# Two transformer blocks on one core: other waits at four stage entries, the GLU's second mean taken of raw squares, and the last norm's weight multiplied before its root is there

## What is computed

```python
def second_block(x, ...):                       # x: (1, 512, 1024)
    h = rms_norm(x, norm_mix_pre)               # x itself is the first block's final rmsnorm
    q, k, v, glu_in, gates = split(h @ w_in)
    a = dilated_attention(q, k, v, rel_bias)    # 3 groups of 4 heads, merged
    c_val, c_gate = split(glu_in)
    c = causal_depthwise_conv(c_val * sigmoid(c_gate), 31 taps)
    c = silu(layer_norm(c))
    mixed = g_a * (a @ w_attn_out) + g_c * (c @ conv_pw_w)
    x = x + rms_norm(mixed @ w_out, norm_mix_post)
    h = rms_norm(x, norm_ffn_pre)
    u = causal_depthwise_conv(h @ w_up, 3 taps)
    f = gelu(u_gate) * u_val
    return x + rms_norm(f @ w_down, norm_ffn_post)

def rms_norm(x, g):
    return x * rsqrt(mean(x * x) + 1e-6) * g
```

## Time and profile before

| | us |
|---|---|
| median of 3 runs | 1909.72 |
| lowest and highest | 1908.21, 1918.91 |
| the profiled execution's own time | 1913.29 |
| its span, first to last instruction | 1911.6 |
| PE busy in the span | 1864.7 (98%) |
| mean granted TensorE clock | 0.991 |

### The profile page before, as it was taken

The page is one execution under the profiler, slowest core; times in us unless marked ns, Lnnn a source line. Parts: engine busy times, 40 slices in busy tenths (PEclk is TensorE's granted clock), DMA queues, the critical chain, the costliest instruction groups (busy, mean ns, idle before and its releaser), DMA issues.

```text
span 1911.6 us, 24566 instructions
## 1 busy us (share of the span) xinstructions
PE 1864.7 (98%) x8540; PEld 1514.4 (79%) x8540; DVE 848.8 (44%) x1505; ACT 725.7 (38%) x1146; POOL 768.0 (40%) x362
## 2 busy tenths in 40 slices
PE   8999999999999999999999999998999889999998
PEld 6777787888877777787878888766788778888887
DVE  5333333343134443343259999925333354545202
ACT  6323323333244444433343243326232364444313
POOL 4434434444443333344434443313344444444442
PEclk9999999999999999999999999999999989999999
DMA  6333332333332322233323433312333323333322
GB/s 183 89 88 82 88 88 75 91 99 88 99 100 88 89 88 88 77 100 88 99 79 97 105 84 88 89 26 69 93 88 108 90 59 94 91 98 99 110 97 90
DMA packets 311966, 174.00 MB, mean 91 GB/s; under 512 B 16368, under 2 KB 304648, under 8 KB 311904
## 3 DMA queue, kind: packets, MB, share of 16 engines
q1 hardware_dynamic: 298960, 165.17, 29.8%
q0 software_dynamic: 2448, 7.93, 1.6%
q10 hardware_dynamic: 10496, 0.07, 0.3%
HBM read 170.95 MB, written 2.20 MB: 91 GB/s over the span
## 4 chain that ended last, share of the span: by engine, by line
PE 93%; DVE 2%; ACT 2%; DMA 2%; issue 0%; SPq 0%; ACTq 0%; DVEq 0%
PE proj L1765 25%; PE proj L1767 24%; PE proj L1766 24%; PE PV L1899 1%; PE A L1867 1%; PE A L2258 1%; PE A L2257 1%; PE A L2256 1%; PE PV L1903 1%; PE A L1873 1%; PE A L1954 1%; PE PV L1954 1%; PE A L1883 1%; DVE A L1452 1%; PE A L1961 1%; PE A L1945 1%
## 5 line engine op out<-in xcount | busy, mean ns | idle before, releaser
L495 POOL TENSOR_TENSOR wlo<-wraw,whi 128x1024 fp32r<-128x1024 f32 (+1 forms) x305 | 722.6, 2372 | 1092.2 <-ACT whi L604 1092.2
L1765 PE MATMUL proj<-Hh,whi 128*128 128x512 f32 x1656 | 667.9, 403 | 9.9 <-DVE ug L1704 4.2
L1767 PE MATMUL proj<-Hh,wlo 128*128 128x512 f32 x1656 | 648.0, 391 | 0.0
L1766 PE MATMUL proj<-Hl,whi 128*128 128x512 f32 x1656 | 647.4, 391 | 0.0
L604 ACT ACTIVATE whi<-wraw 128x1024 fp32r<-128x1024 f32 (+1 forms) x304 | 318.6, 1048 | 771.1 <-DMA wraw<-fox_w_in 183.4
L1765 PEld LDWEIGHTS proj<-Hh,whi 128*128 128x128 f32 x1656 | 312.7, 189 | 81.3 <-issue 7.2
L1766 PEld LDWEIGHTS proj<-Hl,whi 128*128 128x128 f32 x1656 | 312.8, 189 | 69.4 <-issue 6.9
L1767 PEld LDWEIGHTS proj<-Hh,wlo 128*128 128x128 f32 x1656 | 312.4, 189 | 66.6
L1452 DVE SCALAR_TENSOR_TENSOR A<-cin,dwT,A 128x512 f32<-128x512 f32 x232 | 175.1, 755 | 6.8
L1765 PE MATMUL proj<-Oh,whi 128*128 128x512 f32 x256 | 101.1, 395 | 0.7 <-DVE Ol L1253 0.7
L1766 PE MATMUL proj<-Ol,whi 128*128 128x512 f32 x256 | 99.7, 389 | 0.0
(11 more groups left out here) (386 smaller groups left out, 2429.9 us busy)
## 6 DMA issues: line engine op xcount, KB each, us to landing
wraw<-w_in SPq DMA_DIRECT2D x68, 512.0 KB, 3.8
wraw<-fox_w_in SPq DMA_DIRECT2D x57, 512.0 KB, 3.8
wraw<-ret_w_in SPq DMA_DIRECT2D x44, 512.0 KB, 3.8
wraw<-w_up SPq DMA_DIRECT2D x44, 512.0 KB, 3.8
wraw<-w_out SPq DMA_DIRECT2D x40, 512.0 KB, 4.1
wraw<-w_down SPq DMA_DIRECT2D x22, 512.0 KB, 3.5
wraw<-w_mem_kv SPq DMA_DIRECT2D x16, 512.0 KB, 4.1
wraw<-conv_pw_w SPq DMA_DIRECT2D x8, 512.0 KB, 4.1
```

Source lines behind the costliest of these rows:

```text
L495: pool.tensor_tensor(wlo[s][:, 0:r, :], wraw[s][:, 0:r, :], whi[s][:, 0:r, :].bitcast(F32), ALU.subtract).then_inc(w_lo, 1)
L1765: mm(dst, whi[s][:, c, :], xh, start=(first and c == 0), stop=False)
L1766: mm(dst, whi[s][:, c, :], xl, start=False, stop=False)
L1767: ins = mm(dst, wlo[s][:, c, :], xh, start=False, stop=(last and c == chunks - 1))
```

## The change

- **mem1**: `ret_out(HEADS - 1, 1)` moves behind the reading of blocks (0,1) and (0,2).
- **glu**: with v = mean(x*x) + e, the second mean is taken of the raw `acc2`, straight behind the first on PE, into bank A0, before block (0,1). ACT makes 1/v (`rms`) beside r1 = v^(-1/2) (`rms1`); DVE multiplies 1/v by the mean, once. Blocks (1,0) and (1,1) go to banks A2 and PV, which are free, and wait for no reading out.
- **out**: blocks (0,0) and (0,1) are made together: chunks 0 to 2 of the first, 0 to 2 of the second, then chunks 3 to 7 of both in turn. Both blocks' `wlo` are waited for at the start.
- **up**: ACT's `split("up", 0, 1)`, the copy of `whi` for block (2,0), moves ahead of the norm's root. Block (2,0) waits for the reading out of block (0,0) alone.
- **the end**: the halves are multiplied by `gains` in PSUM as soon as each has been squared; the first half's sum becomes y_half = sum/D + e while PE still makes the second; the logarithm takes it as its bias. The last step is one operation a half, y * root + xtok.

```diff
@@ ACT, glu
             act.wait_ge(stats, 2)
             own.mark(f(VT[:], VT[:], ACT.Ln, bias=EPS))
             own.settle()
+            f(rms[:], VT[:], ACT.Exp, scale=-1.0)
             f(rms1[:], VT[:], ACT.Exp, scale=-0.5).then_inc(rms_ready, 1)
-            rms_of(VT, rms, 3)
+            rms_of(rms, rms, 1, sq2_scaled)
@@ ACT, up
             logs()
+            split("up", 0, 1)
             rms_of(VT, rms, 1, x_sq_used)
...
-                    if not (isinstance(i, int) and i == 0 and b == 0):
+                    if not (isinstance(i, int) and i == 0):
                         split("up", i, b, par)
@@ ACT, the end
                     f((sq, sq2)[h][:], y_bank[i][h][:], ACT.Square, accum_out=y_sums[:, 2 * i + h:2 * i + h + 1]).then_inc(y_squared, 1)
+                    if h == 0:
+                        act.wait_ge(y_squared, 2 * i + 1)
+                        own.mark(f(y_half[:, i:i + 1], y_sums[:, 2 * i:2 * i + 1], ACT.Identity, scale=1.0 / D, bias=EPS))
                 act.wait_ge(y_squared, 2 * i + 2)
-                own.mark(f(y_all[:, i:i + 1], y_sums[:, 2 * i:2 * i + 1], ACT.Identity, bias=y_sums[:, 2 * i + 1:2 * i + 2]))
                 own.settle()
-                own.mark(f(y_logs[:, i:i + 1], y_all[:, i:i + 1], ACT.Ln, scale=1.0 / D, bias=EPS))
+                own.mark(f(y_logs[:, i:i + 1], y_sums[:, 2 * i + 1:2 * i + 2], ACT.Ln, scale=1.0 / D, bias=y_half[:, i:i + 1]))
@@ DVE, mem1
                 if before == "ret":
                     ret_out(HEADS - 2, 0)
-                    ret_out(HEADS - 1, 1)
...
                     dve.tensor_copy(vT[:, 0:NMEM], proj[ph.bank(2)][:, 0:NMEM]).then_inc(evac, 1)
+                if before == "ret":
+                    ret_out(HEADS - 1, 1)
@@ DVE, glu
+            own.settle()
+            dve.sem_inc(sq2_summed, 1)
             dve.wait_ge(rms_ready, 3)
-            own.mark(tt(acc2[:], acc2[:], rms1[:], ALU.mult))
-            own.settle()
-            tt(acc2[:], acc2[:], rms1[:], ALU.mult).then_inc(sq2_scaled, 1)
+            dve.wait_ge(stats, 3)
+            tt(rms[:], rms[:], A[0][:], ALU.mult).then_inc(sq2_scaled, 1)
@@ DVE, the end
             for i in range(NT):
+                for h in range(2):
+                    y, at = y_bank[i][h][:], slice(h * S, (h + 1) * S)
+                    dve.wait_ge(y_squared, 2 * i + h + 1)
+                    own.mark(tt(y, y, gains[:, at], ALU.mult))
+                own.settle()
                 dve.wait_ge(y_rooted, i + 1)
                 for h in range(2):
                     y, at = y_bank[i][h][:], slice(h * S, (h + 1) * S)
-                    own.mark(stt(y, y, y_roots[:, i:i + 1], gains[:, at], ALU.mult, ALU.mult))
-                    own.settle()
-                    tt(xtok[:, i, at], xtok[:, i, at], y, ALU.add).then_inc(o_dve, 1)
+                    stt(xtok[:, i, at], y, y_roots[:, i:i + 1], xtok[:, i, at], ALU.mult, ALU.add).then_inc(o_dve, 1)
@@ PE, glu
             statistics(2 * KC)
+            pe.wait_ge(sq2_summed, 1)
+            statistics(2 * KC, A[0], acc2)
             products("glu", 0, 1, 1, H)
-            pe.wait_ge(sq2_scaled, 1)
-            statistics(2 * KC, VT, acc2)
             for b in range(2):
-                products("glu", 1, b, b, H, par=1)
+                products("glu", 1, b, b, H, par=1, bank=(A[2], PV)[b], free=0)
@@ PE, out
-            products("out", 0, 0, 0, (Gh, Gl, 0), each=lambda c: pe.wait_ge(m_lo, c + 1))
-            products("out", 0, 1, 1, (Gh, Gl, 0))
+            ob2 = PH["out"]
+            pe.wait_ge(w_lo, ob2.n(0, 1) + 1)
+            for b, c in ((0, 0), (0, 1), (0, 2), (1, 0), (1, 1), (1, 2), *((b, c) for c in range(3, KC) for b in range(2))):
...
+                if c == 0:
+                    pe.wait_ge(evac, ob2.g(0, b) - 1)
+                pe.wait_ge(m_lo, c + 1)
...
+                if c == KC - 1:
+                    ins.then_inc(w_used, 1)
@@ PE, up
-                    products("up", i, b, b, H, par=i % 2)
+                    products("up", i, b, b, H, par=i % 2, free=PH["up"].g(0, b) + 1 if i == 2 else None)
```

19 lines of the change are left out of this document (12 added, 7 removed).

## The result

| | before | changed |
|---|---|---|
| first series, median (6 runs each) | 1909.77 | 1897.43 |
| second series, median (17 and 6 runs) | 1910.09 | 1895.80 |
| all runs of all series, median | 1911.98 (93 runs) | 1896.39 (12 runs) |
| the runs of these two series alone, median | 1909.82 (23 runs) | 1896.39 (12 runs) |
| profiled execution, and its span | 1913.29, 1911.6 | 1897.74, 1896.0 |

The ratio is 0.9926 (95% interval 0.9906 to 0.9946) in the first series and 0.9918 (0.9899 to 0.9938) in the second: faster, by more than the 0.5% that a measurement can tell. As times these ratios are 14.1 and 15.7 us, each within 3.8. The third row of the table has 15.6 us between its two medians, but it compares across series: 70 of the 93 runs of before belong to series without the changed kernel, where before had medians of 1911.9 to 1913.9. Forecast were 1893.9 and a range of 1889.5 to 1902.0.

What follows compares the result with a forecast made beforehand. PE's matmul work, busy 98% of the span, was taken as the bound, so only PE's waits count. 2.8 + 4.7 + 0.5 + 6.3 + 1.5 = 15.8 us off 1909.72 gives 1893.9; range 1889.5 to 1902.

Steps and rivals of the forecast that it cites:

- mem1, 2.8: At mem1's block (0,3): the `km` copy comes earlier, so PE goes on at 797.13 against 799.91, 2.8 us gained.
- glu, 4.7: At glu's block (1,0): the 2.99 us wait goes and with it 1.75 us of slow clock, 4.7 us gained.
- The delay by POOL's subtraction: At glu: a POOL subtraction (2.4 us) getting in first would delay `rms` to 975.9; PE would still not wait.
- out, 0.5: At out: the 0.99 us wait for `Gl` goes, waits of 0.15 and 0.35 come in, net 0.5 us gained.
- up, 6.3: At up: 4.06 us of wait and 3.04 of slow clock go, a new 0.75 us wait comes, net 6.3 us.
- The 0.75 us wait at block (2,1): At up: POOL ends this block's weights at 1562.8 and PE wants them at 1562.1, a new wait of 0.75 us.
- The end, 1.5: At the kernel's end: the last operations end at 1907.6 instead of 1909.15, with the weight product as bound, 1.5 us gained.
- Slow clock stays: Rival at glu and up: slow clock stays or comes back, taking back 4.8 us, giving 1898.7; chance 0.12.
- A load holds ACT: Rival at up: a load taking 5.9 us instead of 3.9 holds ACT, giving 1895.9 to 1898.9; chance 0.10.
- Given back at dil's end: Rival: the 3.8 us wait at dil's end grows by 1.2 to 4.7 us, giving 1895.1 to 1898.6; chance 0.08.
- Slower: Rival at up's loop: short waits keep PE at the low clock, 25.3 us lost from 128 matmuls on, 1919.2; chance 0.03.
- a large place fails: Rival: a wait stays through another condition, say at up, losing 6.3 us, giving 1900.2; chance 0.07.

Runs made afterwards that it cites:

- up alone: The kernel before with only up's part (`whi` copy ahead of the root, block (2,0) waiting for block (0,0)'s reading out alone): 1907.4 us, ratio 0.9973.

## Why the forecast held, and where it was off

**mem1, 2.8.** Measured 2.8 as a mean, in part by luck. The step "Behind the 2.70 us wait there was no such stretch" was read from one trace; in two of seven there was one, worth 1.6 us, some 0.5 us of gain that the term leaves out. Against it, five of the seven traces with the part lose 0.6 to 0.7 us to the slowed DVE operation at wo0 or wo1, and one of the seven without. The traces that have neither, four without the part (940.9) and two with it (938.2), differ by 2.7: the wait itself was sized rightly.

**glu, 4.7.** Measured 5.0 between the two traces and 5.8 as a mean. The chain on ACT and DVE ran as it was put: `rms` was ready 5.5 us after the start of the first mean (972.05, 966.52), forecast 5.8 (973.5, 967.66). The clock's share was sized at 1.75 from one trace, against a product of 5.44 us; it is 1.6 or 2.8. The other 0.5 us of the 5.8 lie in the wait at dil's end, 3.6 us as a mean in the five traces without the part and 3.1 in the four with it; so few traces don't tell whether that is a draw. The delay by POOL's subtraction, considered under the Trainium skill's page SBUF — State Buffer (shared port pair), did not occur: POOL began at 973.77, after the last product. The DVE operation at wo1 shows that rule at work in this kernel: 2.83 us when it started 0.11 us behind POOL, 0.69 when it was first. That blocks (1,0) and (1,1) have banks of their own was not tried apart; the reading out at 972.34 was ahead of PE's start at 973.72, so by the trace the old bank would have done for block (1,0).

**out, 0.5.** Measured 0.7 to 0.8. The wait for `wlo` at the start, 0.15, did not come. The one for `Y` cost 0.34 us from start to start, where 0.35 was worked out. The wait for `Gl` was taken at its listed 0.99, from the end of a record; from start to start it cost 0.16 more.

**up, 6.3.** Measured 6.2 for up alone (352.8 against a mean of 359.0 in the three traces with the long slow stretch). The clock's 3.04 compares a stretch of rows 5 that reaches into the transposition with a product of 5.44; with the transposition on both sides it is 2.6 to 2.9 in those three traces and 1.4 in two others. The 0.75 us wait at block (2,1) was mis-sized: it was 0.18. POOL's `wlo` was ready 8.9 us after the start of the root's logarithm, forecast 9.0; but PE asked for it only 8.9 us after, forecast 8.3, since block (2,0) began 0.2 us later and took 6.17 us with its transposition instead of 5.84. The small one at block (2,0), 0.20 where 0.1 was put, came from POOL's `wlo`, as forecast, though the view names `uv` (see the rows at up). Three conditions on one block was the right reading: with ACT's copy put back, 4.6 us are lost.

**The end, 1.5.** 1.5 in the trace. The product with the weight is the step behind which the last two operations wait, as said.

**The rivals.** Slow clock stays: it did not stay in glu and up; but one appeared in mix behind the 2.05 us wait of the first changed trace (8.73 us at 0.80, against 7.15 at 1.00 in the second), so "No wait of up to 2.70 us on this trace led to slow clock" held for that trace and not for others. The new short waits, for which it was used, did have no slow stretch behind them. A load holds ACT: ACT did wait for the landing, but the root's logarithm came 1.26 us after the mean's matmul where it had come 1.05 us after, 0.2 us later and not 0.35, and the load landed 3.96 us after its issue. Given back at dil's end: 3.8 before, 3.7 after, and 2.4 to 4.1 over all traces in which it is unfilled, not longer with the change (2.4 to 3.7) than without (2.8 to 4.1). *Slower* and *a large place fails* did not come.

```profile
1326.38:1335.11 8.73, 7.34 (x25) 5.56 (x25) 4.02 (x3) 0.00 (x0) 2.19 (x1) 0.80 0.01 3
```

```profile
1324.75:1331.90 7.15, 5.77 (x24) 4.42 (x24) 4.03 (x3) 0.00 (x0) 2.19 (x1) 1.00 0.01 3
```

**The total.** Between the two profiled spans the gain is 15.6 us and forecast were 15.8, but draws stand in that difference: the late clock at the start (-2.3), the slow stretch in mix (-1.6), and the 2.5 us in dil's last turn, which stay unexplained. The ratios give 14.1 and 15.7, each within 3.8, and the stretches 16.8; 15.8 fits all three, and none of them can tell it from 14 or 17. The changed kernel's first median, 1897.4, is 3.5 us above the forecast. That cannot be put on one step: the level of 1909.72 was a median of three runs, of a kernel whose single runs go from 1906 to 1919 and whose series have medians from 1909.8 to 1913.9, and the gain between the medians of 6 runs was 12.3.

## What to carry to other kernels

Where matmul work fills 98% of the time, cost a wait of PE as its length plus the slow clock that may stand behind it, and take the second part as a draw: look at the same wait in several traces before you size it. A faster PE is worth time only where PE is the bound in that stretch; before adding work to hold the clock, compare the stretch's length at either level. When a wait has several conditions, look at when each of them ended, since the view names the last record and not the condition. And set a forecast of 1% on a median of many runs, not of three, and compare kernels within one series.

## What the runs showed of the hardware that I had not expected

- The clock behind one and the same wait differs between executions of one program: behind 2.70 us there was none in five traces and a slow stretch in two; behind 2.05 us a slow one in four of eleven; behind 2.99 us the product of 5.4 to 5.6 us took 7.2 in three and 8.35 in two. In the 12 runs of before it goes with the time, 1.8 us for each 0.001 of mean clock.
- Matmuls of constants, whose results nobody reads, hold the clock: a mean of 0.998 to 1.000 in place of 0.994 to 0.995 with four waits filled. Idle rests of 0.5 and 0.8 us in the filled waits at glu and up were followed by full clock; a rest of 2.0 us in dil's last turn was followed by 22.6 us at 0.92.
- One f32 matmul of 128x248 is two instructions, 0.43 us together, while one of 128x512 on the rounded halves takes 0.23.
- A DVE operation and a POOL subtraction that both read SBUF do not share: the one that starts first takes its usual time and the other is held. At wo0 or wo1 the DVE operation took 2.77 to 2.83 us, in place of 0.69, when POOL was 0.11 to 0.17 us ahead (six traces). When DVE was 0.07 to 0.34 us ahead (20 such pairs in the 14 traces), it took its 0.69 and POOL 2.61 to 2.88 us in place of 2.4, ending 2.94 us after DVE's start each time.
